# A multi-layer sequence model on one core: the MLP's two matrix products by seven half products for eight

## What is computed

```python
def sq_relu_mlp(h, w1, w2):
    return jnp.square(jax.nn.relu(h @ w1)) @ w2
...
        x = x + g1 * y
        x = x + g2 * sq_relu_mlp(modulate(x, norm2_g[l], sh2, sc2), w_mlp1[l], w_mlp2[l])
```

## Time and profile before

| | |
|---|---|
| median of three runs | 4362.51 us (4362.19 to 4364.94) |
| span of the profiled execution | 4364.0 us |
| TensorE matmul busy | 4013.5 us, 92% |
| VectorE, ScalarE, GpSimd busy | 1530.0, 944.2, 577.8 us |
| first MLP matmul to the last, in the trace | 1516.8 to 2401.0 us |

### The profile page before, as it was taken

How to read it: one execution, slowest core, us unless ns; L and a number is a source line. 1 busy time by engine, 2 the same in 40 slices (tenths; PEclk the granted TensorE clock), 3 DMA queues, 4 the chain that set the end, 5 groups by cost and what they waited for, 6 DMA issues and landing times.

```text
span 4364.0 us, 51611 instructions
## 1 busy us (share of the span) xinstructions
PE 4013.5 (92%) x21278; PEld 2527.3 (58%) x21278; DVE 1530.0 (35%) x3530; ACT 944.2 (22%) x1814; POOL 577.8 (13%) x603
## 2 busy tenths in 40 slices
PE   5897997988999999999999897899989998799899
PEld 3477995576467444444444456885554557775454
DVE  2573553235444101111113644531162363621341
ACT  4122331222100200000002411320252310320341
POOL 3002331023000110000002201211000101201001
PEclk7996998988999999999999999999999999999999
DMA  5201002035345111111110312211100312211100
GB/s 189 102 5 26 25 25 88 25 104 180 101 156 203 39 39 39 39 39 39 37 36 28 125 30 73 73 40 51 54 1 25 140 36 57 76 59 39 44 25 39
DMA packets 215480, 278.17 MB, mean 64 GB/s; under 512 B 24333, under 2 KB 174056, under 8 KB 214352
## 3 DMA queue, kind: packets, MB, share of 16 engines
q1 hardware_dynamic: 201904, 206.17, 15.1%
q0 software_dynamic: 13344, 68.70, 4.2%
HBM read 240.03 MB, written 34.81 MB: 63 GB/s over the span
## 4 chain that ended last, share of the span: by engine, by line
PE 85%; DVE 7%; issue 3%; ACT 2%; DMA 2%; POOL 1%; SPq 0%; POOLq 0%; DVEq 0%; ACTq 0%
PE ps L805 16%; PE ps L2748 10%; PE ps L2762 10%; PE ps L2658 8%; PE ps L827 7%; PE ps L3417 6%; PE ps L3699 4%; PE ps L2419 3%; PE ps L3910 2%; PE ps L3893 1%; PE ps L851 1%; DVE big L3512 1%; PE ps L1475 1%; PE ps L1459 1%; DMA big<-hs_scratch 1%
## 5 line engine op out<-in xcount | busy, mean ns | idle before, releaser
L805 PE MATMUL ps<-big 128*128 128x512 f32 (+1 forms) x1760 | 685.6, 551 | 2.8 <-DMA big<-hs_scratch 2.8
L805 PEld LDWEIGHTS ps<-big 128*128 128x128 f32 x1760 | 335.6, 192 | 343.7 <-issue 334.4
L2748 PE MATMUL ps<-big 128*128 128x512 f32 x1024 | 442.3, 594 | 8.6 <-issue 8.6
L2762 PE MATMUL ps<-big 128*128 128x512 f32 x1024 | 440.8, 592 | 0.0
L2812 DVE SCALAR_TENSOR_TENSOR big<-ps,big 128x512 f32<-128x512 f32 x128 | 96.0, 750 | 776.8 <-PE ps L2762 776.8
L2658 PE MATMUL ps<-big 128*128 128x512 f32 (+1 forms) x896 | 359.3, 562 | 3.0 <-DVE big L4028 2.0
L2748 PEld LDWEIGHTS ps<-big 128*128 128x128 f32 x1024 | 195.1, 191 | 254.2 <-issue 254.2
L2762 PEld LDWEIGHTS ps<-big 128*128 128x128 f32 x1024 | 194.6, 190 | 244.9 <-issue 244.9
L827 PE MATMUL ps<-big 128*128 128x256 f32 (+1 forms) x1792 | 319.2, 341 | 12.5 <-DVE big L1909 10.1
L827 PEld LDWEIGHTS ps<-big 128*128 128x128 f32 x1792 | 288.3, 194 | 43.9 <-DVE big L1909 10.3
L2658 PEld LDWEIGHTS ps<-big 128*128 128x128 f32 x896 | 169.6, 190 | 187.6 <-issue 180.8
(11 more groups left out here) (458 smaller groups left out, 5256.4 us busy)
## 6 DMA issues: line engine op xcount, KB each, us to landing
big<-in_w_mlp SPq DMA_DIRECT2D x32, 1024.0 KB, 5.4
big<-in_w_in SPq DMA_DIRECT2D x29, 1024.0 KB, 5.2
big<-in_w_mod SPq DMA_DIRECT2D x24, 1024.0 KB, 5.3
big<-in_w_ada SPq DMA_DIRECT2D x24, 1024.0 KB, 6.3
big<-us_scratch SPq DMA_DIRECT2D x72, 256.0 KB, 4.4
hs_scratch<-big POOLq DMA_DIRECT2D x3, 5120.0 KB, 16.8
big<-c_dft SPq DMA_DIRECT2D x12, 1024.0 KB, 5.7
xs_scratch<-big POOLq DMA_DIRECT2D x16, 640.0 KB, 3.5
```

The lines of the kernel that those rows point to most:

```text
L805: t = e.matmul(b[:, 0:n], wv[:, k, 128 * m:128 * m + 128], K.hT[:, k, t0:t0 + n], start=(k == 0), stop=(k == 7))
L2748: t = e.matmul(b[:, :], wv[:, k, 128 * m:128 * m + 128], K.hT[:, k, t0:t0 + n], start=(k == 0), stop=(k == 7))
L2762: t = e.matmul(b[:, :], wv[:, k, 128 * m:128 * m + 128], h[:, k, t0:t0 + n], start=(k == 0), stop=(k == 3))
```

## The change

Both layers' products are worked as 2 x 2 blocks by seven block products. The weight tile W is cut in four corners W[i][j] (i: half of its outputs, j: half of the contraction), the input in X[j][l] (l: token half). GpSimd makes three sums of weights in buffers and one in place, VectorE the same of the inputs. A bank a collects P1, P6, P7 and P2 one after the other and is read between them; b holds one product, d two. The first pass of layer one and all of the last step (2, 7) keep the eight products.

The diff, cut:

```diff
         self.gcol = K.m6(5)
+        tail, mem = Arena(K.big, M0 + 8192, M0 + 10240), K.spare()
+        self.xs = [mem.get(4, 512) for _ in range(3)]
+        more = Arenas([tail, mem])
+        self.ws = [[more.get(512) for _ in range(3)] for _ in range(2)]
+        edge = K.hT0[:, :, T:TT]
+        flat = [mem.get(512) for _ in range(2)]
+        self.hs = [[edge[:, 4 * i + 2 * k:4 * i + 2 * k + 2, :] for k in range(2)] for i in range(2)]
+        self.hs.append([x.rearrange("p (a b) -> p a b", a=2) for x in flat])
 
...
+    def whole(self, which, g, half):
+        return (which, g, half) == (1, 0, 0) or (which, g) == (2, 7)
+    def slots(self):
+        n = 0
+        for u, (which, g, half) in enumerate((w, g, half) for w, g in self.order() for half in range(2)):
+            if not self.whole(which, g, half):
+                yield u, n, which, g, half
+                n += 1
+    def corner(self, which, s, i, j):
+        if which == 1:
+            return s[:, 4 * j:4 * j + 4, 128 * i:128 * i + 128]
+        return s[:, 2 * j:2 * j + 2, 256 * i:256 * i + 256]
...
+    def seven(self, e, P, pr, which, g, half, m, n, wv, *keys):
+        a, b, d = (("mlp", which, g, half, m, x) for x in "abd")
+        W = [[self.corner(which, wv, i, j) for j in range(2)] for i in range(2)]
+        X = [[self.input_corner(which, g, j, l) for l in range(2)] for j in range(2)]
+        S1, S2, S4 = self.weight_sums(which, n)
+        c = slice(128 * m, 128 * m + 128)
...
+            return t
+        made = (lambda q: ("mlp", "input sum", q)) if which == 1 else (lambda q: ("mlp", "hidden sum", g, q))
+        T1, T2, T4 = self.xs if which == 1 else self.hs
+        pr.open(e, a)
+        product(a, W[0][0], X[0][0], True).then_inc(P.sem, P.up(("mlp", "P1", a)))
+        pr.open(e, b)
+        product(b, W[0][1], X[1][0], True).then_inc(P.sem, P.up(("mm", b)))
+        e.wait_ge(*self.at("mlp", "weight sum", n, 2))
+        e.wait_ge(*self.at(*made(2)))
+        e.wait_ge(*self.at("mlp", "P1 out", a))
+        product(a, S2, T2, False).then_inc(P.sem, P.up(("mlp", "P16", a)))
+        pr.open(e, d)
+        product(d, S1, T1, True).then_inc(P.sem, P.up(("mlp", "P5", d)))
+        e.wait_ge(*self.at("mlp", "weight sum", n, 3))
+        e.wait_ge(*self.at(*made(3)))
+        e.wait_ge(*self.at("mlp", "P16 out", a))
+        product(a, W[1][0], X[0][1], False).then_inc(P.sem, P.up(("mlp", "P167", a)))
+        e.wait_ge(*self.at("mlp", "weight sum", n, 4))
+        e.wait_ge(*self.at("mlp", "P5 out", d))
+        product(d, S4, X[1][1], False).then_inc(P.sem, P.up(("mm", d)))
+        e.wait_ge(*self.at(*made(4)))
+        e.wait_ge(*self.at("mlp", "P167 out", a))
+        product(a, W[1][1], T4, False).then_inc(P.sem, P.up(("mm", a), ("mlp", "sums used", n), *keys))
...
     def tensor(self, e):
         K, P = self.K, self.sig("tensor")
...
         for which, g in self.order():
             h = self.h[g % 2]
             if which == 1:
                 for half in range(2):
                     used, wv = K.W.use(e, 256)
-                    for m in range(2):
-                        for t0, n in BLKS[0:2]:
+                    if not self.whole(1, g, half):
+                        self.seven(e, P, pr, 1, g, half, 0, numbers[1, g, half], wv, used, ("mlp", "done", 1, g))
+                        continue
+                    for t0, n in BLKS[0:2]:
+                        for m in range(2):
                             u = ("mlp", 1, g, half, m, t0)
                             b = pr.open(e, u)
                             for k in range(8):
                                 K.normal(e, t0, k)
                                 t = e.matmul(b[:, :], wv[:, k, 128 * m:128 * m + 128], K.hT[:, k, t0:t0 + n],
                                              start=(k == 0), stop=(k == 7))
-                            t.then_inc(P.sem, P.up(("mm", u), used, ("mlp", "done", 1, g)))
+                            t.then_inc(P.sem, P.up(("mm", u), used, ("mlp", "whole")))
                 continue
-            e.wait_ge(*self.at("mlp", "squared", g))
+            e.wait_ge(*self.at("mlp", "squared", g, "scalar"))
+            e.wait_ge(*self.at("mlp", "squared", g, "vector"))
+            if g < 7:
+                for half in range(2):
+                    used, wv = K.W.use(e, 512, 4)
+                    for m in range(2):
+                        self.seven(e, P, pr, 2, g, half, m, numbers[2, g, half], wv, used, ("mlp", "done", 2, g))
+                continue
             ws = []
             for half, m, i in self.second(g):
                 if len(ws) == half:
...
-                for m in range(2):
-                    for t0, n in BLKS[0:2]:
-                        u = ("mlp", 1, g, half, m, t0)
-                        e.wait_ge(*self.at("mm", u))
-                        e.activation(self.h[g % 2][:, 2 * half + m, t0:t0 + n], self.bank(u)[:, :], ACT.Relu).then_inc(
-                            S.sem, S.up(("free", u, 0), ("mlp", "relu", u)))
+                if self.whole(1, g, half):
+                    for l, (t0, n) in enumerate(BLKS[0:2]):
+                        for m in range(2):
+                            u, h = ("mlp", 1, g, half, m, t0), self.tile(g, half, m, l)
+                            e.wait_ge(*self.at("mm", u))
+                            e.activation(h, self.bank(u)[:, :], ACT.Relu).then_inc(S.sem, S.up(("free", u, 0)))
+                            e.wait_ge(S.sem, S.n)
+                            e.activation(h, h, ACT.Square).then_inc(S.sem, S.up(("mlp", "squared", g, "scalar")))
+                    continue
+                a, b, d = (("mlp", 1, g, half, 0, x) for x in "abd")
+                e.wait_ge(*self.at("mlp", "P1", a))
+                e.activation(self.tile(g, half, 0, 0), self.bank(a)[:, :], ACT.Copy).then_inc(
+                    S.sem, S.up(("mlp", "P1 out", a)))
+                e.wait_ge(*self.at("mlp", "P16", a))
+                e.activation(self.tile(g, half, 0, 1), self.bank(a)[:, :], ACT.Copy).then_inc(
+                    S.sem, S.up(("mlp", "P16 out", a)))
+                e.wait_ge(*self.at("mlp", "P5", d))
+                e.activation(self.tile(g, half, 1, 1), self.bank(d)[:, :], ACT.Copy).then_inc(
+                    S.sem, S.up(("mlp", "P5 out", d)))
+                h = self.tile(g, half, 1, 0)
+                e.wait_ge(*self.at("mm", a))
+                e.activation(h, self.bank(a)[:, :], ACT.Relu).then_inc(S.sem, S.up(("free", a, 0)))
+                e.wait_ge(S.sem, S.n)
+                e.activation(h, h, ACT.Square).then_inc(S.sem, S.up(("mlp", "squared", g, "scalar")))
         for half, m, i in self.second(7):
...
     def gpsimd(self, e):
         G = self.sig("gpsimd")
...
+        e.wait_ge(*self.at("sum", "rms4c", 0))
+        for u, n, which, g, half in self.slots():
+            u += self.base
+            s = self.K.W.slots[u % len(self.K.W.slots)].rearrange("p (k c) -> p k c", k=8 if which == 1 else 4)
+            W = [[self.corner(which, s, i, j) for j in range(2)] for i in range(2)]
+            S1, S2, S4 = self.weight_sums(which, n)
+            e.wait_ge(*self.at("weights", "in", u))
+            if n >= 2:
+                e.wait_ge(*self.at("mlp", "sums used", n - 2))
+            e.tensor_tensor(S1, W[1][0], W[1][1], ALU.add).then_inc(G.sem, G.up())
+            e.wait_ge(G.sem, G.n)
+            e.tensor_tensor(S2, S1, W[0][0], ALU.subtract).then_inc(G.sem, G.up(("mlp", "weight sum", n, 2)))
+            e.tensor_tensor(W[1][0], W[0][0], W[1][0], ALU.subtract).then_inc(
+                G.sem, G.up(("mlp", "weight sum", n, 3)))
+            e.wait_ge(*self.at("mlp", "weight sum", n, 2))
+            e.tensor_tensor(S4, W[0][1], S2, ALU.subtract).then_inc(G.sem, G.up(("mlp", "weight sum", n, 4)))
         for half, m, i in self.second(7):
             for x in self.sums:
                 x.add(e, G, i, 4 * half + m)
 
...
+    def input_sums(self, e, V):
+        X = [[self.input_corner(1, 0, j, l) for l in range(2)] for j in range(2)]
+        T1, T2, T4 = self.xs
+        for i in range(2):
+            for k in range(8):
+                e.wait_ge(*self.at("normal", "rms2", i, k))
+        e.tensor_tensor(T1, X[0][1], X[0][0], ALU.subtract).then_inc(V.sem, V.up())
+        e.wait_ge(V.sem, V.n)
+        e.tensor_tensor(T2, X[1][1], T1, ALU.subtract).then_inc(V.sem, V.up(("mlp", "input sum", 2)))
+        e.wait_ge(V.sem, V.n)
+        e.tensor_tensor(T4, X[1][0], T2, ALU.subtract).then_inc(V.sem, V.up())
+        e.wait_ge(*self.at("mlp", "whole"))
+        e.tensor_tensor(X[0][1], X[1][1], X[0][1], ALU.subtract).then_inc(
+            V.sem, V.up(("mlp", "input sum", 3), ("mlp", "input sum", 4)))
+    def hidden_sums(self, e, V, g):
+        X = [[self.input_corner(2, g, j, l) for l in range(2)] for j in range(2)]
+        T = self.hs
+        e.wait_ge(*self.at("mlp", "squared", g, "scalar"))
```

(113 more changed lines are left out.)

7 lines of the change are left out of this document (removed).

## The result

The changed kernel takes 4267.5 us, the median of four runs (4263.2 to 4272.5), against 4362.7 for the kernel before; the ratio is 0.978 (95% interval 0.9765 to 0.9792). In a second comparison it was 0.977 (0.9757 to 0.9784). The forecast, 4262.9 of 4362.5, was a ratio of 0.977.

A forecast was written before the change was run, and what follows sets the result against it. TensorE's unbroken matmuls were taken to bound the MLP; removed calls save 99.6 us, all other terms cost 0, so 4362.5 - 99.6 = 4262.9 us as a median, 8-in-10 range 4258 to 4285.

The forecast's parts named there:

- The matmuls removed: MLP, both layers: 29 passes lose 4 calls each, 116 calls at 0.858 us, so 99.6 us less.
- The hand-overs: New TensorE waits on bank a (60 layer one, 112 layer two): round trip 1.01 us, layer-two slack 0.28, cost 0.
- rival A: Layer-two waits on bank a each 0.30 us late, 34 us more, 4297 us; chance 0.14 together with Rival D.
- VectorE, ScalarE, GpSimd, the start: MLP: added sums, squarings and PSUM reads, and the input sums at its start, all hidden behind TensorE, cost 0.
- Rival B: Layer-two waits 0.6 us late, TensorE's idling lowers its clock to 0.93: 119 us more, 4382 us; chance 0.04.
- Rival C: GpSimd's sums bound the MLP: at 7 us a sum nothing is gained, 4362 us or slightly more; chance 0.01.
- Rival D: MLP calls get longer: 0.1 us more for each block product, 4293 us; chance 0.14 together with rival A.

## Why the prediction was right

**The matmuls removed.** Right in size and reason: 0.858 us a call, steps of 48.07 us, 99.62 us less in the MLP. The groups of two calls and the moving operand in two runs cost nothing.

**The hand-overs.** The outcome, no stall, was right, but two terms of the working were wrong. The slack is 0.55 us and not 0.28, because a late weight load costs about 0.15 us and not the 0.43 of its lead. And 84 hand-overs of layer two count, not 112. Both errors made the change look more fragile than it is; rival A at its price of 34 us would need evictions about 0.95 us longer by the measured terms, and not 0.58.

**VectorE, ScalarE, GpSimd, the start.** All hidden, as forecast. Only the contention was under-priced: 1.46 to 1.70 us an operation in four of the hidden sums for 1.33. As the later ones ran undisturbed, all seven together took 8.6 us (1666.2 to 1674.8), inside the 10.3 of the forecast and a cover of 17 us. The first three input sums took 3.2 us each beside GpSimd, and not 2.4; only the fourth, alone, took 2.3. The first three were ready at 1533.8, between the forecast's 1532.2 and its 1539.4 for a doubling, and nobody waited. That layer one has 2 us of slack was not tried; the runs show only that it has no stall. The start was not moved, but I read the 8.60 us ahead of it as given; its cause was in the text, and the way out was one line.

**Rival B** stood on a wrong price. I took the granted clock by the share of idle time in other stages: 0.93 at 9.3%, 0.56 at 25%. The runs show 1.00 with 56 idle pieces of up to 0.5 us, 0.96 and 0.89 with 34% and 27% of a step idle in pieces up to 3.5 us, and 0.87 with 21% idle in 29 pieces up to 9.4 us. So the share alone does not set it; share and length were not varied one at a time, so what does is open. The Trainium skill tells of a bf16 kernel whose clock swings through micro-idles between matmul groups that go round the banks (TensorE: Matmul & The Clock Gate, "A second HAM failure mode: psum-queue depth-cycling"). The pieces of up to 0.5 us in this float32 kernel did not do that: the clock stayed at 1.00. **Rival C** had the right break-even in kind: GpSimd is no bound at 12 sums a pass and is at 24. **Rival D** fell with the 48.07 us.

**The median.** The trace's gain was exact, and the median came out 4.6 us above the forecast, inside the range. The scatter of both kernels, some 10 us, belonged in the range from the start and was read too small from three runs. That the median hit to 5 us is in part luck: the kernel before had a median of 4362.7 in one comparison and 4368.0 in the next.

## What to carry to other kernels

Where one engine fills a stage without a gap, the gain of taking work from it is count times duration, and the real question is whether each new wait has a cover longer than its round trip. Count only the waits that stand one behind another, and take the round trip from the timeline; an idle time marked "issue" with no releaser, just ahead of such a stage, is worth asking which buffer the first instruction opens. When whole runs scatter by 10 us, compare the stage in the trace: it repeated to 0.01 us.

## What was not expected of the hardware

A weight load released late costs TensorE about 0.15 us before its matmul, although such loads otherwise start 0.43 us ahead. Copies of 256 columns on VectorE that each wait for the one before follow at 0.53 us, where one takes 0.42 us. TensorE idling a third of a step, in pieces of up to 3.5 us, had a granted clock of 0.96 in one step, while another step with 27% idle had 0.89; behind the same pause of 3.51 us eight records took 3.67 us once and 5.37 us in the next set. A VectorE sum of 2048 elements and a GpSimd sum of 512, all inputs in SBUF, take 3.2 to 3.3 us each side by side, and 2.29 and 1.26 us alone.
